# The feed-forward part in seven half-size products instead of eight (Strassen's scheme, Winograd's form)

## The reference

```
n  = rms_norm(x);  q, k, v, indexer, u = split(n @ w_in)
a  = sparse attention over the top 128 (prompt) or 256 (sampled, paged cache) keys
c  = conformer convolution (GLU, depthwise 31 taps, layer norm, silu)
h  = x + concat(a, c) @ w_out                       # 2048 x 2048
n2 = rms_norm(h, norm_ffn)
h  = h + (silu(n2 @ w_gate) * (n2 @ w_up)) @ w_down # 2048 x 5632 twice, 5632 x 2048
y  = rms_norm(h, norm_final)
```

## Time and profile before

| | |
|---|---|
| runs | 2508.98, 2515.99, 2512.28 us; median 2512.28 |
| profiled execution, span | 2507.0 us |
| TensorE busy | 2459.3 us (98%) |
| VectorE busy | 1391.1 us (55%) |
| ScalarE busy | 832.8 us (33%) |
| GpSimd busy | 383.4 us (15%) |
| DMA, mean | 102 GB/s, 255.11 MB |

### The profile page before, as it was taken

One profiled execution on the slowest core, in us unless ns is written; L12 is line 12 of the kernel. 1 busy time (PEld: TensorE's weight loads), 2 busy tenths in 40 slices (PEclk: granted clock), 3 DMA queues, 4 the chain that ended last, 5 costly groups with the idle time before them and its releaser, 6 DMA issues.

```text
span 2507.0 us, 46035 instructions
## 1 busy us (share of the span) xinstructions
PE 2459.3 (98%) x17064; PEld 2290.0 (91%) x17066; DVE 1391.1 (55%) x2382; ACT 832.8 (33%) x1091; POOL 383.4 (15%) x430
## 2 busy tenths in 40 slices
PE   7999999999999999999999999999999999999999
PEld 6968999996679999999999999999999999999998
DVE  6688989996334464444444444544444444444565
ACT  6153344325332243333223333223333322222233
POOL 2334899623610000000000000000000000000000
PEclk9999999999999999999999999999999999999999
DMA  7414222315873342322232322233322223322232
GB/s 248 123 36 115 76 84 83 90 44 164 277 210 106 107 125 86 90 86 71 87 110 84 92 84 74 85 100 93 92 84 82 75 86 109 89 87 84 69 92 95
DMA packets 424732, 255.11 MB, mean 102 GB/s; under 512 B 19980, under 2 KB 413444, under 8 KB 423969
## 3 DMA queue, kind: packets, MB, share of 16 engines
q1 hardware_dynamic: 412864, 224.91, 30.8%
q0 software_dynamic: 11792, 29.23, 3.5%
HBM read 243.66 MB, written 11.27 MB: 102 GB/s over the span
## 4 chain that ended last, share of the span: by engine, by line
PE 86%; issue 3%; DVE 3%; POOL 3%; ACT 2%; DMA 1%; SPq 0%; DVEq 0%; POOLq 0%; ACTq 0%
PE ps L1618 46%; PE ps L1622 23%; PE ps L1603 10%; POOL y L589 3%; PE ps L1892 1%; PE ps L1722 1%; PE ps L1866 1%; PE ps L1739 1%; PE ps L1912 1%; ACT tap L774 1%; PE ps L1848 1%; DMA xN<-in_x_prompt 0%; ACT whi L648 0%; PE ps L2010 0%; PE ps L1941 0%
## 5 line engine op out<-in xcount | busy, mean ns | idle before, releaser
L1618 PE MATMUL ps<-xs,whi 128*128 128x320 f32 (+2 forms) x4992 | 1100.3, 329 | 2.3 <-DVE wlo L999 1.6
L999 DVE TENSOR_TENSOR wlo<-raw,whi 128x1024 fp32r<-128x1024 f32 (+1 forms) x366 | 447.8, 1225 | 871.0 <-ACT whi L648 866.5
L648 ACT CAST whi<-raw 128x1024 fp32r<-128x1024 f32 (+1 forms) x410 | 429.1, 1048 | 985.5 <-PE ps L1622 753.9
L1618 PEld LDWEIGHTS ps<-xs,whi 128*128 128x128 f32 x4992 | 742.4, 189 | 3.0 <-issue 2.0
L1622 PE MATMUL ps<-xs,wlo 128*128 128x320 f32 (+1 forms) x3328 | 689.5, 289 | 0.0
L1622 PEld LDWEIGHTS ps<-xs,wlo 128*128 128x128 f32 x3328 | 503.6, 188 | 64.7
L1618 PE MATMUL ps<-hs,whi 128*128 128x320 f32 (+2 forms) x2046 | 451.2, 329 | 1.0 <-DVE ut L1509 1.0
L1603 PE MATMUL ps<-xs,whi 128*128 128x272 f32 (+1 forms) x2368 | 396.1, 289 | 7.2 <-DVE xs L1007 3.1
L1603 PEld LDWEIGHTS ps<-xs,whi 128*128 128x128 f32 (+1 forms) x2368 | 334.4, 187 | 10.0 <-DVE xs L1007 3.6
L1618 PEld LDWEIGHTS ps<-hs,whi 128*128 128x128 f32 x2046 | 304.2, 189 | 1.8 <-issue 1.0
L1622 PE MATMUL ps<-hs,wlo 128*128 128x320 f32 x1364 | 282.6, 289 | 0.0
(11 more groups left out here) (323 smaller groups left out, 1782.1 us busy)
## 6 DMA issues: line engine op xcount, KB each, us to landing
raw<-in_w_gate SPq DMA_DIRECT2D x88, 512.0 KB, 3.7
raw<-in_w_up SPq DMA_DIRECT2D x88, 512.0 KB, 3.7
raw<-in_w_in SPq DMA_DIRECT2D x72, 512.0 KB, 3.6
raw<-in_w_down SPq DMA_DIRECT2D x64, 384.0 KB, 3.3
raw<-in_w_down SPq DMA_DIRECT2D x64, 320.0 KB, 3.1
raw<-in_w_out SPq DMA_DIRECT2D x32, 512.0 KB, 5.3
ring_pages<-in_cache_k SPq DMA_DIRECT2D x40, 128.0 KB, 3.5
ring_pages<-in_cache_k POOLq DMA_DIRECT2D x40, 128.0 KB, 3.6
```

The lines of the kernel that those rows point to most:

```text
L648: nc.scalar.copy(whi[:, u.slot, :, 0:cols], raw[:, u.slot, :, 0:cols]).then_inc(s_hi, 1)
L999: ve.tensor_tensor(wlo[:, u.slot, :, 0:cols], raw[:, u.slot, :, 0:cols], whi[:, u.slot, :, 0:cols].bitcast(F32), ALU.subtract).then_inc(s_ ...
L1618: te.matmul(ps[:, bank, 0:c1 - c0], whi[:, u.slot, t, :], both[:, c0:c1], start=(hf == 0 and t == 0), stop=(hf == 1 and t == k - 1 and ban ...
```

## The change

The FFN's matrix products are cut in two along each axis and done by Winograd's form of Strassen's scheme: seven products of half-size blocks with sums of blocks before and after. The contraction is halved, the 544 tokens are halved (272), and the output columns are halved by pairing: gate with up for one hidden tile, and two neighbouring output tiles in down.

- **Activations.** From `hg` seven operands `opX` are made once (blocks of 8 K-tiles x 272 tokens, four of them sums, made by GpSimd in `operand_sums`), each split high and low, in 13 pieces.
- **Weights.** For a pair of tiles four blocks of raw weights come by DMA (`wr1`, double-buffered, `wr2` for down). Besides the blocks themselves (three are used raw) four sums are needed. GpSimd makes two, `ws1 = b2 + b3` and `b2 = b0 - b2`; VectorE makes two in place, `b0 = ws1 - b0` behind the low part of product 0 and `b1 = b1 - b0` behind that of product 2. All seven are split high (ScalarE) and low (VectorE) into slots of which three or four are in turn.
- **Products.** Each has 8 K-steps (4 or 6 in down), three matmuls of 272 columns a K-step, all into one PSUM bank. Products 3 to 5 and 6 add onto what products before have left in the bank, after a copy of it has been taken out.
- **Gate/up.** 44 pairs in a loop of two, with ScalarE copies and VectorE adds out of PSUM. The hidden tile is not split at once: GpSimd forms the seven operands' sums for two hidden tiles together (`hid_sums`), SP stores them to DRAM.
- **Down.** All 44 hidden tiles' gate/up work comes first, then down in four chunks of 4, 6, 6, 6 K-steps (`KG`), written out in full. SP loads seven operands a chunk, which are split again, in nine places in turn. Eight gathers a pair add PSUM onto `h`.
- **h** no longer stays in SBUF during gate/up. The output projection stores each tile to DRAM, and it is loaded when down begins.

```diff
+BLOCK = (0, None, 1, 0, 1, 2, 3)
+BANK = ((0, 6, 1, 0, 6, 0, 1), (2, 7, 3, 2, 7, 2, 3))
+SLOT1 = (0, 1, 2, 0, 1, 2, 3)
+BACK1 = (4, 4, 4, 3, 3, 3, 7)
# TensorE
+            def product(n, par, i, whi_, wlo_, op, kk, ready=None):
+                pe.wait_ge(s_wlo, fed(n, i))
+                for t in range(kk):
+                    if ready is not None:
+                        pe.wait_ge(s_opl, ready(t))
+                    for w, x in ((whi_, 0), (whi_, 1), (wlo_, 0)):
+                        ins = te.matmul(prod_bank(par, i), w[:, t, :], op[:, x, t, :],
...
+                ins.then_inc(s_prod, 1)
+                for i in range(7):
+                    if i in (3, 4, 5):
+                        pe.wait_ge(s_tc, 4 * n + i - 2)
+                    if i == 6:
+                        pe.wait_ge(s_te, 4 * n + 1)
# GpSimd
+            def weight_sum1(par, k, n, fill):
+                if k == 0:
+                    pool.wait_ge(s_wr[par], AT_WR + 64 * fill)
+                    dst, x, z, op = ws1, raw4[2], raw4[3], ALU.add
+                    if not first:
+                        pool.wait_ge(s_wlo, fed(n - 1, 1))
+                        pool.wait_ge(s_wdif, 2 * n - 1)
+                else:
+                    dst, x, z, op = raw4[2], raw4[0], raw4[2], ALU.subtract
...
+            weight_sums1(1, 1, 1)
+            weight_sums1(0, 2, 2)
+            hid_sums(0)
+            with pool.Fori(1, NB2 - 1) as m:
+                weight_sums1(1, 2 * m + 1, m + 1)
+                weight_sums1(0, 2 * m + 2, m + 2)
+                hid_sums(m)
# ScalarE, one gate/up pair
+                taken(t1[:, 0:HALF], par, 0, n)
+                weight_high1(par, 3, n, fill)
+                taken(t2[:, HALF:NT], par, 1, n)
+                weight_high1(par, 4, n, fill)
+                weight_high1(par, 5, n, fill)
+                weight_high1(par, 6, n, fill)
+                taken(t1[:, HALF:NT], par, 3, n)
+                nxt(0)
+                nxt(1)
+                gate_silu(n)
+                taken(t2[:, 0:HALF], par, 5, n)
+                nxt(2)
# VectorE
+            def weight_low1(par, i, n):
+                dve.wait_ge(s_whi, fed(n, i))
+                ve.tensor_tensor(w[:, 1, :, :], src[:, :, :], w[:, 0, :, :].bitcast(F32), ALU.subtract).then_inc(s_wlo, 1)
+                if i == 0:
+                    dve.wait_ge(s_wsum, 2 * n + 2)
+                    dve.wait_ge(s_wlo, fed(n, 0))
+                    ve.tensor_tensor(raw4[0][:, :, :], ws1[:, :, :], raw4[0][:, :, :], ALU.subtract).then_inc(s_wdif, 1)
+                elif i == 2:
+                    dve.wait_ge(s_wdif, 2 * n + 1)
+                    dve.wait_ge(s_wlo, fed(n, 2))
+                    ve.tensor_tensor(raw4[1][:, :, :], raw4[1][:, :, :], raw4[0][:, :, :], ALU.subtract).then_inc(s_wdif, 1)
+            def pair1(par, n, nxt, extra=None, last=False):
+                weight_low1(par, 3, n)
+                weight_low1(par, 4, n)
+                weight_low1(par, 5, n)
+                added(t1[:, 0:HALF], t1[:, 0:HALF], par, 2, n, 1)
+                weight_low1(par, 6, n)
+                nxt(0)
+                added(t1[:, HALF:NT], t1[:, HALF:NT], par, 4, n, 3)
+                ve.tensor_tensor(t1[:, :], t1[:, :], rstd2[:, :], ALU.mult).then_inc(s_ts, 1)
+                nxt(1)
+                ve.tensor_tensor(t2[:, HALF:NT], t2[:, 0:HALF], t2[:, HALF:NT], ALU.add).then_inc(s_te, 1)
+                nxt(2)
+                added(t2[:, 0:HALF], t2[:, 0:HALF], par, 6, n, 4)
+                ve.tensor_tensor(t2[:, :], t2[:, :], rstd2[:, :], ALU.mult).then_inc(s_us, 1)
+                ve.tensor_tensor(hid[par][:, :], t2[:, :], t1[:, :], ALU.mult).then_inc(s_hid, 1)
# VectorE, down: product v of pair p, chunk c, i = p % 8
+                        gathered(p, v)
+                    x = v + 3
+                    if p + x // 7 < 4 * NP2:
+                        weight_low2(p + x // 7, x % 7)
+                    if c < 3 and i in (5, 6) and v == 6:
+                        operand_low(c + 1, i - 5)
+                    if c < 3 and i == 7 and v >= 3:
+                        operand_low(c + 1, v - 1)
+                    if c and i == 0 and v == 0:
+                        operand_low(c, 6)
+                    if c == 3 and v == 1 and i:
+                        final(2 * i - 1)
+                    if c == 3 and v == 6 and not last:
+                        final(2 * i)
# SP
+            with sp.Fori(1, NB2 - 1) as m:
+                sp.wait_ge(s_wlo, fed(2 * m - 1, 6))
+                load_pair1(2 * m + 1, 1)
+                store_odd(m - 1)
+                sp.wait_ge(s_wlo, fed(2 * m, 6))
+                load_pair1(2 * m + 2, 0)
+                store_even(m)
...
+            store_odd(NB2 - 1)
+            sp.wait_ge(s_prod, fed(NP1 - 1, 6))
+            sp.dma_start(h[:, 0:2, :], xT_dram[:, 0:2, :]).then_inc(s_xr[0], 16)
```

More of the change, by code:

```diff
@@ L61 @@
 UK = 8
-CH, CJ = 4, 11
-DK = (6, 5)
+KH = KT // 2
+NP1 = DFF // P
+NB2 = NP1 // 2
+NP2 = KT // 2
+KG = (4, 6, 6, 6)
+KG0 = (0, 4, 10, 16)
+KM = 6
+NPIECE = 13
+AT_OPD = AT_HL = 32 * 6
+AT_WR = 32 * 8
+AT_XW = AT_HO = 16 * (16 // 2)
 P_QI = 0
@@ L494, in _ @@
                     if q % 2:
[L495 to L513 removed]
+                        s = q // 2
@@ new lines, in gate_silu @@
+            def gate_silu(n):
+                act.wait_ge(s_ts, n + 1)
+                nc.scalar.activation(t1[:, :], t1[:, :], ACT.Silu).then_inc(s_silu, 1)
+            with act.Fori(0, 4) as i:
+                out_highs(i)
+            piece_high(0)
+            piece_high(1)
+            out_highs(4)
+            for x in range(2):
+                act.wait_ge(s_xd, x + 1)
+                piece_high(2 + x)
+            with act.Fori(5, 7) as i:
+                out_highs(i)
+            weight_high1(0, 0, 0, 1)
@@ L969, in rows_left @@
+            nc.scalar.activation(stat[:, 62:63], stat[:, 0:1], ACT.Sqrt)
             def rows_left(i, kb):
@@ new lines, in _, with added @@
+            with dve.Fori(5, 7) as i:
+                out_pair(i)
+            dve.wait_ge(s_mm, 2 * M_FFN - 2)
+            residual(14, 0, 16 * 8)
+            for i in range(3):
+                weight_low1(0, i, 0)
+            piece_low(4)
+            piece_low(5)
+            dve.wait_ge(s_mm, 2 * M_FFN)
+            residual(15, 1, 16 * 8)
+            for x in range(6, 9):
+                piece_low(x)
+            def added(dst, base, par, i, n, before):
+                dve.wait_ge(s_prod, fed(n, i))
+                dve.wait_ge(s_tc, 4 * n + before)
+                ve.tensor_tensor(dst, prod_bank(par, i), base, ALU.add).then_inc(s_te, 1)
@@ new lines, in _ @@
+            pair1(0, 0, True)
+            pair1(1, 1)
+            with pe.Fori(1, NB2) as m:
+                pair1(0, 2 * m)
+                pair1(1, 2 * m + 1)
+            for p in range(4 * NP2):
+                c = p // NP2
+                n = NP1 + p
+                if p < 2:
+                    pe.wait_ge(s_te, 4 * n - 4)
+                else:
+                    pe.wait_ge(s_hacc, 8 * (p - 1))
+                for i in range(7):
+                    if i >= 3:
+                        pe.wait_ge(s_hacc, 8 * p + (1, 2, 4, 3)[i - 3])
+                    if p % NP2 == 0:
+                        pe.wait_ge(s_opl, NPIECE + 7 * c + i + 1)
+                    product(n, p % 2, i, wh2[(7 * p + i) % 3], wl2[(7 * p + i) % 3], opH[op_slot(c, i)], KG[c])
```

674 lines of the change are left out of this document (471 added, 203 removed).

## The result

The changed kernel takes 2432.43 us (median of four runs, 2426.76 to 2435.85) against 2513.44 for the kernel before in the same job: a ratio of 0.9672, interval 0.9655 to 0.969. Forecast was 2415, range 2345 to 2495. The profiled execution has a span of 2433.9 us against 2507.0, 73.1 less where the sum said 97.

What follows compares the result with a forecast made beforehand. TensorE was taken to bound the FFN. Matmuls -193, gate/up exclusion +32, start +8, hand-over +8, down +48 give -97 us; from the 2507.0 span, plus 5.3, 2415 us, range 2345 to 2495.

Steps and rivals of the forecast that it cites:

- the lock: VectorE operations with two SBUF inputs and GpSimd operations exclude each other; one stands until the other's is over.
- The race: Odd gate/up pairs: VectorE's multiply or GpSimd's weight sum goes first, costing 0.1 to 2.5 us a double pair; 32 us taken.
- tail: After the last product: keeps its form, 0 us (-1 to 2).
- part 1: FFN matmuls: 11,088 of 272 columns at 0.125 us, an eighth of the columns gone at unchanged column price; -193 us.
- rival 4: FFN matmuls: accumulating into one bank is slower than alternating, 9 ns more each, +100 us, 2515 us; chance 0.04.
- part 2: Gate/up: whether the other engines keep up with TensorE; mutual exclusion costs 1.5 us a double pair, 32 us (2 to 84).
- part 3: Start of the FFN: late low parts and splits cost 8 us (3 to 15); output projection 0 (to 3).
- the four-slot ring of 5.95 us units covers that: Output projection: the weight ring hides the few us per pair that added h stores keep SP; 0 us (to 3).
- part 4: Hand-over from gate/up to down: h's load behind stores delays VectorE's first gather and low parts; 8 us (4 to 15).
- part 5: Down: early operand splits, chunk changes and a nearly full VectorE in the last chunk cost 48 us (15 to 85).
- rival 1: VectorE and GpSimd find gaps, TensorE stays the bound; ten gate/up pairs take 210 us, total 2352 us; chance 0.22.
- Rivals 2 and 3: In gate/up: chain closes badly every double pair, 4 us each, 2489 us, chance 0.15; weight sums delay every pair, 2594, 0.06.

## Why the prediction was right, and where its sizes were off

The time fell inside the range and near the forecast, 17 us above it, and the mechanism held: an eighth of the columns goes, and the lock and the edges take part of it back. That the sum came so near is partly luck. The race's 32 us, which did not come, stood in for 45 us of loss at the output projection, the start and the hand-over that the sum lacked; three of those terms lie above or at the top of their ranges, and the race's lies below its own. In us, against the kernel before; the products' share is 7392 at 0.126 and 3696 at 0.125:

| term | predicted | measured |
|---|---|---|
| matmuls | -193 | -185 |
| output projection | 0 (to 3) | +14 |
| start of the FFN | +8 (3 to 15) | +32 |
| race in odd gate/up pairs | +32 (2 to 84) | +0.4 |
| hand-over, with down's first pair | 8 + 2 | +17 |
| rest of down | 46 | +50 |
| tail | 0 | -1 |
| sum | -97 | -73 |

**Matmuls (part 1): right, 8 us off.** An eighth of the columns went and the price of a column stayed. In ten pairs 1680 matmuls took 211.7 us, 126.0 ns each; in down's chunk 1 five pairs of 126 x 5 = 630 took 78.7, 124.9. One bank for 12 or 18 matmuls in a row costs nothing in down (10.5 us for 84 in chunk 0 are 125.0 ns), and 24 in a row in gate/up at most the 1 ns, so rival 4, which needed 9, is out. What adds this 1 ns is open: it is there with GpSimd's busy time at 12% instead of 35% too, and neither the 24 in a row nor the operands' layout was tried by itself.

**The race (part 2): the mechanism right, the size wrong.** The lock, the order of the work and the moment at which GpSimd's sum is ready were as worked out, and with two more sums on GpSimd the chain closed in just the odd pairs, at 2.5 us each. But I took 1.5 us between 0.1 and 2.5, that is a mixture of the race's two outcomes, and in this profile all 21 were won, by 0.3 to 1.1 us. The hidden tile came at 4.5 in the odd pair, not 5.3, and that 0.8 put the multiply ahead. The price of a won race was too high as well: L3 ended at 7.9, not 9.0.

The margin is real but thin, since the sum starts when its DMA has landed. In the eight profiles with unchanged gate/up work four odd pairs were longer than 21.18 us, by 0.1 to 0.8. In them the sum came 5.2 to 5.9 us into the pair and stood ahead of L3, as in this one of 21.93 (final scale on ScalarE, pair begins at 1739.06):

```profile
1745.06 7.84 DVE L1837 TENSOR_TENSOR wp<-wr,wp 128x1024 fp32r<-128x1024 f32 x3 [1.45 <-ACT wp L1169]
```
```profile
1744.94 2.40 POOL L808 TENSOR_TENSOR ws<-wr,wr 128x1024 f32<-128x1024 f32 x1 [14.04 <-DMA wr<-in_w_up]
```

The multiply itself was ahead in all 168 odd pairs of these eight profiles, by 0.2 us at least; what a late load costs is the sum in front of L3.

**Output projection (part 3): the step failed.** I said that "the four-slot ring of 5.95 us units covers that". It did not look at what stands behind a store. SP already stood 137 us in this stage for tiles of `h` before the change (126 after it), with the weights of a unit later behind that wait; new is the store on its way to DRAM in each half iteration, in the one shown 2.24 us from its issue to the residual's load. The row that spoke against the cover was in rows 7: before the change ScalarE already waited 59.4 us for those loads; now it waits 95.2.

**Start (part 3): the places right, the size a quarter.** The late weights (7.2) I had not seen, since they come from the same queue. In the first pair the late splits, the wide GpSimd sum and the reciprocal are the ones named, but I left out that VectorE has a single gap of 0.7 us from 934 to 966 in which to catch up, and that GpSimd blocks it for 9 us there: 7.36 us for three splits that need 2.84, 6.84 for two that need 2.48. And the granted clock is 0.75 in that stretch, a mean of its two levels (1.2 and 2.4 GHz), so that products between two idles take longer. The first two products, 48 matmuls, in the changed kernel (granted clock 0.80 in them) and with SP's queue reordered (1.00):

```profile
928.52 7.68 PE L2456 MATMUL ps<-opX,wp 128*128 128x272 f32 x48 [7.21 <-issue]
```
```profile
907.73 6.22 PE L2466 MATMUL ps<-opX,wp 128*128 128x272 f32 x48
```

So TensorE's idle time was paid for twice: of the 32 us, 23 are idle and some 8 are products that took longer. In down it was so too: 483 us busy for 462 us of matmuls.

**Hand-over (part 4): right in kind.** The wait for `h` is the one described; the other, for a late operand, was not named. Together they cost 17 us against 10, 12.6 of them idle and the rest products at a granted clock of 0.69.

**Down (part 5): the sum right, partly by luck.** Chunk changes 38 us (34 in the next profiles), for 31 with the early operands; last chunk 12, for 14. For the last chunk, luck is the word: what part 5 called exclusive there, 18.3 us less the 3.5 of gathers that may lie beside GpSimd, fits into 15.75, and the 2 us a pair were picked. That the lock makes this loss is shown by the last chunk without it: no loss, with more work on VectorE.

**The lock.** By the Trainium skill ("SBUF — State Buffer", Who interferes with whom) a VectorE instruction with two SBUF inputs contends with a GpSimd instruction that reads SBUF, and the second to issue "fully blocks". The durations agree: with four sums on GpSimd a multiply of 0.73 us became 2.61 beside a sum. What I missed is that a blocked instruction is recorded as busy, so that busy times taken beside the other engine are no measure of work, and that work can be moved *onto* the busier engine with a gain.

Of the other signs named ahead: ten pairs took 211.7 us, near rival 1's 210 and not the forecast's 217, so that in gate/up rival 1 held; in down, where it had 28 us with the hand-over, 67 were lost. The gap ahead of the first product was 7.2 us, under the 15 named. GpSimd's busy time rose by 499 us where the sum of its new work was 394. I had called far more than 394 a proof against the prediction; it was a bad sign to choose, since 26 us of the surplus are the start's operand sums, which the 394 left out, and the rest is blocked time, as the mean of 3264 for 2403 shows. Rivals 2 and 3 needed a loss in every double pair or every pair, and there was none.
